# Entry to the convolution stage: a gate half scaled out of its bank into SBUF, two weight roundings moved behind a sigmoid, and the spread of the norm's factor two k steps earlier

## The chip, the cores and the metric

One core of one Trainium2 chip runs the whole program once. The metric is the device time in microseconds, the median of the runs shown. TensorE does matmuls, VectorE (DVE), ScalarE (ACT) and GpSimd (POOL) do elementwise work, and SyncE (SP) only issues the DMAs that bring weights.

## The reference

Two transformer-like blocks on 512 tokens of width 1024, in float32. The change touches the entry of each phase that begins with a root-mean-square norm, and above all the start of the conformer convolution:

```python
def conformer_conv(h, w_pw1, b_pw1, w_dw, b_dw, ln_g, ln_b, w_pw2, b_pw2):
    u = h @ w_pw1 + b_pw1                # 1024 -> 2048
    a, g = jnp.split(u, 2, axis=-1)
    u = a * jax.nn.sigmoid(g)
    u = depthwise_conv(u, w_dw) + b_dw   # 31 taps along the tokens
    u = jax.nn.silu(layer_norm(u, ln_g, ln_b))
    return u @ w_pw2 + b_pw2

# in the layer: h = rms_norm(x, gain); x = x + rms_norm(conformer_conv(h, ...), gain)
```

## The kernel before

Activations lie transposed, 128 channels by 512 tokens to a tile, eight tiles to a tensor. Every float32 product is made of three matmuls with rounded parts: the high part of the weight with the high and with the low part of the activation, and the low part of the weight with the high part (L1646, L1647, L1648). A k step of a tile is one such triple, and a tile of TensorE is eight k steps, 24 matmuls.

Weights come in blocks of 128x1024. For block n, SP loads `raw` once `w_lo` says that the block four back is done on GpSimd; ScalarE rounds it to the high part `wh` (`hi`, L631), once TensorE has finished the block four back (`blocks_done`); GpSimd subtracts and gets the low part `wl` (`lo`, here L528); then TensorE may use the block (`open_block` waits for `w_lo`). All rings have four places. Results go round PSUM banks 0 to 3: tile T waits until tile T-4 has been released by VectorE (`open_tile`, `bank_free`).

A phase with a norm begins with `enter` on TensorE: its first three tiles run interleaved over k, as the operand's pieces arrive, and the fourth follows as a whole. The norm is not applied to the operand but to the results. During the fourth tile, hooks put in the sum of squares (`stat`, ahead of k step 1) and, ahead of k step 5, `spread`, which spreads the factor (`rcol`, from VectorE's reciprocal, L1081) over all partitions in PSUM. ScalarE copies it to `r2` (`keep_r2`, L663), and VectorE multiplies results by `r2`. The kernel has five entries with hooks: the first MLP tiles of both layers, the convolution stage `pw1`, and two in the second block.

`pw1` works in the order of the list `PW1`: a0, g0, a1, g1, then for each j from 2 to 7: a_j, c_(j-2), g_j, and at the end c6, c7. a_j and g_j are the two halves of the projection for 128 channels, c_j is eight of the 31 taps as matmuls with diagonal weights. n0 is the first block of the stage, T0 its first tile, one block to each entry of the list. Each engine has its own program, in an order written out by hand:

- VectorE, for each j: `gate(j)` scales a_j (in place, in its bank) and g_j (into `tmp[:, 1]`, which signals `gate_z`) by `r2`, combines c_(j-2), and with the sigmoid makes U(j) (L1409). Then `taps(j)`: 18 taps (L1422 to L1434, by helpers at L1056 and L1060). The first of them releases the banks of both halves (2 for j<2, 3 after that, with c_(j-2)).
- ScalarE: for each g in the list the sigmoid (L879), the high part UH(j) (L883), then roundings of blocks up to four or five places ahead (L884, L885), and then five products for GpSimd's taps (L898). Before the list, `enter` (L689) rounds blocks n0+4 to n0+7.
- GpSimd: after `lo_to(n0 + 7)` (L569), for each j: the low part UL(j) (L556), blocks, tap additions (L539), blocks, tap additions, a running sum (L546), vector-tap additions (L567), blocks.
- TensorE: tile c0 is preceded by ten filler matmuls (L1656) and waits for UH(0) and UL(0).

Of the kernel before, what the change touches and what calls it, by code (L numbers as in the profile page):

```python
# [27 lines left out]
ALU = mybir.AluOpType  # L28
# [85 lines left out]
PW1_BLOCK, PW1_TILE = {}, {}  # L114
# [16 lines left out]
def build(nc, x_t, meta_t, positions, vectors, weights, out_t):  # L131
    ctx = ExitStack()
    with ctx:
        def sb(name, shape, dt=F32):
            return ctx.enter_context(nc.sbuf_tensor(name, shape, dt))

        def sem(name):
            return ctx.enter_context(nc.semaphore(name))
# [11 lines left out]
        tmp = sb("tmp", [P, 2, S])  # L150
# [3 lines left out]
        r2 = sb("r2", [P, S])  # L154
# [88 lines left out]
        PS = ctx.enter_context(nc.psum_tensor("PS", [P, 8, S], F32))  # L243
# [17 lines left out]
        def col(name, i=0):  # L261
            return vec[:, COL[name] + i:COL[name] + i + 1]
# [18 lines left out]
        blocks_done = sem("blocks_done")  # L281
        bank_free = sem("bank_free")
# [333 lines left out]
        def _(sc):  # L616
# [7 lines left out]
            def hi(n):  # L624
                if n >= NBLK:
                    return
                j = n % RING
                sc.wait_ge(raw_in[j], 16 * (n // RING + 1))
                if n >= RING:
                    sc.wait_ge(blocks_done, n - RING + 1)  # L630
                sc.activation(wh[:, j], raw[:, j], ACT.Copy).then_inc(w_hi, 1)  # L631
# [57 lines left out]
            def enter(phase, entry):  # L689
                n0 = BLOCK0[phase]  # L690
                hi(n0 + 4)
                root(entry)
                hi(n0 + 5)
                keep_r2(entry)
                hi(n0 + 6)
                hi(n0 + 7)
# [174 lines left out]

            boundary("x2")
            n0 = BLOCK0["pw1"]
            enter("pw1", "x2")
            done = n0 + 8
            for i, (kind, j) in enumerate(PW1):
                if kind == "g":
                    sc.wait_ge(gate_z, j + 1)
# [7 lines left out]
                done = max(done, upto)  # L886
# [30 lines left out]
            n0 = BLOCK0["w_in_2"]  # L917
# [91 lines left out]
            n0 = BLOCK0["ffn_up"]  # L1009
# [27 lines left out]
        def _(v):  # L1037
            chain = [0]

            def step(ins):  # L1040

                chain[0] += 1
                ins.then_inc(dve, 1)
                v.wait_ge(dve, chain[0])
# [6 lines left out]
            def tt(out, a, b, op):  # L1051
                return v.tensor_tensor(out, a, b, op)  # L1052

            def ts(out, a, s1, op0, s2=None, op1=None):
                if op1 is None:
                    return v.tensor_scalar(out, a, s1, None, op0)  # L1056
                return v.tensor_scalar(out, a, s1, s2, op0, op1)
# [93 lines left out]
            T0, n0 = TILE0["w_in"], BLOCK0["w_in"]  # L1151
# [215 lines left out]
            T0, n0 = TILE0["pw1"], BLOCK0["pw1"]  # L1367
# [26 lines left out]
            def gate(j):  # L1394

                b = j % 2
                Ta, Tg = T0 + PW1_TILE[("a", j)], T0 + PW1_TILE[("g", j)]
                a = PS[:, Ta % 4]
                v.wait_ge(blocks_done, n0 + PW1_BLOCK[("a", j)] + 1)
                step(tt(a, a, r2[:], ALU.mult))  # L1400
                v.wait_ge(blocks_done, n0 + PW1_BLOCK[("g", j)] + 1)
                tt(tmp[:, 1], PS[:, Tg % 4], r2[:], ALU.mult).then_inc(gate_z, 1)
                if j >= 2:
                    conv_out(j - 2)
                v.wait_ge(gate_s, j + 1)
                if j >= 2:
                    v.wait_ge(uh_done, j - 1)
                    v.wait_ge(ul_done, j - 1)
                sig(stt(U[:, b, PAD:PAD + S], a, col("b_pw1", j), sqb[:, 0], ALU.add, ALU.mult), u_done, j + 1)  # L1409

            def taps(j):

                b, first, end = j % 2, PE_TAPS, TAPS - POOL_TAPS
                Tg = T0 + PW1_TILE[("g", j)]
                base = chain[0]
                if j:
                    v.wait_ge(dve_taps, 2 * j)
                for t in range(first, end):
                    a = PS[:, (RB, HB)[t % 2]]
                    w, src = col("w_dw", j * TAPS + t), U[:, b, t:t + S]  # L1420
                    if t == first:
                        ts(a, src, w, ALU.mult).then_inc(bank_free, 2 if j < 2 else 3)  # L1422
                        continue
                    if t == first + 1:
                        ts(a, src, w, ALU.mult).then_inc(dve, 1)
                        continue
                    if t == first + 2:
                        v.wait_ge(bank_free, Tg + 1)
                    else:
                        v.wait_ge(dve, base + t - 2 - first)  # L1430
                    if t < end - 2:
                        stt(a, src, w, a, ALU.mult, ALU.add).then_inc(dve, 1)
                    else:
                        stt(taps_sum[:, b, t % 2], src, w, a, ALU.mult, ALU.add).then_inc(dve_taps, 1)  # L1434
                chain[0] += end - 3 - first
# [27 lines left out]
            T0, n0 = TILE0["w_in_2"], BLOCK0["w_in_2"]  # L1463
# [153 lines left out]
            T0, n0 = TILE0["ffn_up"], BLOCK0["ffn_up"]  # L1617
# [19 lines left out]
            T0, n0 = TILE0["ffn_down"], BLOCK0["ffn_down"]  # L1637
# [5 lines left out]
        def _(pe):  # L1643
# [22 lines left out]
            def stat(job):  # L1666

                n = JOB[job]
                pe.wait_ge(ssq_adds, SSQ_ADDS[n])
                if n:  # L1670
                    pe.wait_ge(sd_done, n)
                if job == "meta":
                    pe.matmul(PS[0:META, STAT, 0:1], ssq[:, 0:META], ones[:, 0:1], start=True, stop=True).then_inc(stat_done, 1)
                    return
                for j in range(4):
                    ins = pe.matmul(PS[:, STAT, j:j + 1], ssq[:, j * P:(j + 1) * P], ones[:, 0:1], start=True, stop=True)  # L1676
                ins.then_inc(stat_done, 1)

            def spread(job):

                n = JOB[job]
                pe.wait_ge(rcol_done, n + 1)
                if job == "meta":
                    pe.matmul(PS[:, RB, 0:META], rcol[0:META, n, 0:1].broadcast_to((META, P)), ident[0:META, 0:META],
                              start=True, stop=True).then_inc(rb_done, 1)
                    return
                for j in range(4):
                    ins = pe.matmul(PS[:, RB, j * P:(j + 1) * P], rcol[:, n, j:j + 1].broadcast_to((P, P)), ident[:],  # L1688
                                    start=True, stop=True)
                ins.then_inc(rb_done, 1)  # L1690
# [17 lines left out]
            def enter(phase, operand, hook_job=None):  # L1708

                n0, T0, x0 = BLOCK0[phase], TILE0[phase], KT * OPN[operand]  # L1710
                for k, t in [(k, t) for k in range(KT) for t in range(3)]:
                    if k == 0:
                        open_block(n0 + t)
                        open_tile(T0 + t)
                    if t == 0:
                        pe.wait_ge(xh, x0 + k + 1)
                        pe.wait_ge(xl, x0 + k + 1)
                    ins = products(PS[:, (T0 + t) % 4], *weight(n0 + t, k), XH[:, k], XL[:, k], k == 0, k == KT - 1)
                    if k == KT - 1:
                        ins.then_inc(blocks_done, 1)  # L1720
                hooks = {1: lambda: stat(hook_job), 5: lambda: spread(hook_job)} if hook_job else {}
                tile(n0 + 3, T0 + 3, hooks)

            def norm_out(job, next_phase, before=W_STAT, after=W_UPDATE):
# [57 lines left out]
            def spread_meta():  # L1782
# [3 lines left out]
            hooks = {4: {4: lambda: spread("x0"), 7: lambda: stat("q_lat")}, 5: {5: lambda: spread("q_lat")},  # L1786
                     6: {3: lambda: stat("kv_lat")}, 7: {2: lambda: spread_kv()},
                     9: {2: lambda: stat("meta")}, 12: {2: lambda: spread_meta()}}
# [11 lines left out]
            n0, T0 = BLOCK0["up_q"], TILE0["up_q"]  # L1800
# [4 lines left out]
            n0, T0 = BLOCK0["up_kn"], TILE0["up_kn"]  # L1805
# [4 lines left out]
            n0, T0 = BLOCK0["up_v"], TILE0["up_v"]  # L1810
            open_block(n0)
            for t in range(4):
                open_tile(T0 + t)
                q = slice(t * P, (t + 1) * P)
                for k in range(2):
                    w = [x[:, n0 % RING, 4 * k:4 * k + 4].rearrange("p s m -> p (s m)") for x in (wh, wl)]
# [84 lines left out]
            n0, T0 = BLOCK0["w_out"], TILE0["w_out"]  # L1901
# [38 lines left out]
            n0, T0 = BLOCK0["pw1"], TILE0["pw1"]  # L1940
# [49 lines left out]
            n0, T0 = BLOCK0["w_in_2"], TILE0["w_in_2"]  # L1990
# [46 lines left out]
            n0, T0 = BLOCK0["w_in_2b"], TILE0["w_in_2b"]  # L2037
# [3 lines left out]
            for i in range(4):  # L2041
# [4 lines left out]
                for kk in range(2):  # L2046
                    k = 2 * i + kk
                    w = [x[:, n % RING, 4 * kk:4 * kk + 4].rearrange("p s m -> p (s m)") for x in (wh, wl)]
# [15 lines left out]
            n0, T0 = BLOCK0["w_out_2"], TILE0["w_out_2"]  # L2064
# [5 lines left out]
            n0, T0 = BLOCK0["ffn_up"], TILE0["ffn_up"]  # L2070
# [8 lines left out]
            n0, T0 = BLOCK0["ffn_down"], TILE0["ffn_down"]  # L2079
# [163 lines left out]
```

## Time and profile before

| | us |
|---|---|
| median of 3 runs (1879.87 to 1881.52) | 1880.98 |
| the profiled execution | 1879.82 |
| its span in the profile | 1878.0 |
| TensorE busy | 1820.3 |
| GpSimd busy | 900.8 |
| VectorE busy | 809.6 |
| ScalarE busy | 636.8 |

The span runs from the first to the last instruction; the execution's own time has 1.8 us around it. Busy times are sums over the span of one execution. TensorE's granted clock is 0.985 of full speed over the span. A stretch of the stage in question is 665 to 800 us. Rows of a timeline give start and length in microseconds, engine, line, operation and tiles, and in brackets how long the engine was idle before it and what released it; short idle times have no bracket.

### The profile page before, as it was taken

To read this page: it belongs to the slowest core of one execution; us is meant where nothing else is said; L and a number is where in the kernel's file an instruction comes from. 1 tells how busy PE (TensorE), PEld (TensorE's weight loads), DVE (VectorE), ACT (ScalarE), POOL (GpSimd) and SP (SyncE) were. 2 spreads that over 40 slices of the span, in tenths; PEclk is the share of its full clock that TensorE was granted. 3 is DMA by queue.
4 is the path that set the end of the run, shared out by engine and by line. 5 is a ranking of instruction groups with operands and counts; after the bars stand their busy time and mean duration, and the time that the engine had idled before them with its cause. 6 is when DMAs were issued, how large, how long until landed. Compare 5 with 4: busy or idle time off the path is not lost.

```text
span 1878.0 us, 23679 instructions
## 1 busy us (share of the span) xinstructions
PE 1820.3 (97%) x8511; PEld 1506.6 (80%) x8511; DVE 809.6 (43%) x1238; ACT 636.8 (34%) x954; POOL 900.8 (48%) x478
## 2 busy tenths in 40 slices
PE   7999999999999989999999999998998999999999
PEld 5787887888888768787888888887878778888887
DVE  7447645301321478855520232256546154444200
ACT  5327525222321444444321222252245242222221
POOL 5346445444444479954444444453243354444443
PEclk9999999999999989999999999998999999999999
DMA  5332022233232213221322322310210223322332
GB/s 176 85 121 68 12 90 79 90 101 96 93 101 92 66 56 102 68 88 61 109 95 95 101 91 99 100 57 24 81 57 1 68 68 101 101 94 96 101 103 76
DMA packets 45925, 157.87 MB, mean 84 GB/s; under 512 B 5728, under 2 KB 5984, under 8 KB 45856
## 3 DMA queue, kind: packets, MB, share of 16 engines
q1 hardware_dynamic: 45856, 156.93, 26.4%
q8 instruction: 46, 0.75, 0.2%
q14 instruction: 23, 0.19, 0.0%
HBM read 152.58 MB, written 2.10 MB: 82 GB/s over the span
## 4 chain that ended last, share of the span: by engine, by line
PE 86%; POOL 5%; DVE 5%; issue 2%; ACT 2%; DMA 0%; SPq 0%; POOLq 0%; DVEq 0%; ACTq 0%
PE PS L1646 27%; PE PS L1647 26%; PE PS L1648 26%; POOL acc_p L539 2%; PE PS L1656 2%; POOL wl L528 2%; PE PS L1857 1%; PE PS L1688 1%; PE PS L1676 1%; DVE PS L1060 1%; POOL acc_p L567 1%; PE PS L2017 1%; POOL UL L556 0%; DVE tmp L1060 0%; DVE XL L1052 0%
## 5 line engine op out<-in xcount | busy, mean ns | idle before, releaser
L475 POOL TENSOR_TENSOR wl<-raw,wh 128x1024 fp32r<-128x1024 f32 x232 | 563.0, 2428 | 677.0 <-ACT wh L645 293.1
L1646 PE MATMUL PS<-XH,wh 128*128 128x512 f32 x1408 | 561.2, 399 | 14.8 <-DVE PS L1056 5.0
L1647 PE MATMUL PS<-XL,wh 128*128 128x512 f32 x1408 | 552.3, 392 | 0.0
L1648 PE MATMUL PS<-XH,wl 128*128 128x512 f32 x1408 | 551.9, 392 | 0.0
L1646 PEld LDWEIGHTS PS<-XH,wh 128*128 128x128 f32 x1408 | 267.0, 190 | 78.5 <-issue 12.4
L1648 PEld LDWEIGHTS PS<-XH,wl 128*128 128x128 f32 x1408 | 266.7, 189 | 56.9
L1647 PEld LDWEIGHTS PS<-XL,wh 128*128 128x128 f32 x1408 | 267.0, 190 | 52.6
L1646 PE MATMUL PS<-HH,wh 128*128 128x512 f32 x688 | 267.6, 389 | 0.0
L1647 PE MATMUL PS<-HL,wh 128*128 128x512 f32 x688 | 267.6, 389 | 0.0
L1648 PE MATMUL PS<-HH,wl 128*128 128x512 f32 x688 | 267.6, 389 | 0.0
L645 ACT ACTIVATE wh<-raw 128x1024 fp32r<-128x1024 f32 x96 | 101.6, 1061 | 405.0 <-PE PS L1648 405.0
L1052 DVE TENSOR_TENSOR tmp<-PS,r 128x512 f32<-128x512 f32 x116 | 79.9, 691 | 236.2 <-PE PS L1648 215.9
L631 ACT ACTIVATE wh<-raw 128x1024 fp32r<-128x1024 f32 x94 | 98.6, 1055 | 154.6 <-PE PS L1648 146.0
L1648 PEld LDWEIGHTS PS<-HH,wl 128*128 128x128 f32 x688 | 129.1, 188 | 26.8
L1646 PEld LDWEIGHTS PS<-HH,wh 128*128 128x128 f32 x688 | 129.1, 188 | 26.8
L1647 PEld LDWEIGHTS PS<-HL,wh 128*128 128x128 f32 x688 | 129.1, 188 | 26.8
L466 POOL TENSOR_TENSOR wl<-raw,wh 128x1024 fp32r<-128x1024 f32 x33 | 80.5, 2446 | 131.1 <-ACT wh L631 131.0
L864 ACT ACTIVATE wh<-raw 128x1024 fp32r<-128x1024 f32 x56 | 59.4, 1060 | 164.2 <-PE PS L1648 164.2
L1031 ACT ACTIVATE wh<-raw 128x1024 fp32r<-128x1024 f32 x40 | 42.5, 1062 | 159.0 <-PE PS L1648 159.0
L496 POOL TENSOR_TENSOR prob<-prob,cols 128x512 f32<-128x512 f32 (+2 forms) x64 | 57.5, 901 | 64.4 <-DVE cols L1266 64.1
L1356 DVE COPY M<-PS 128x512 f32 x16 | 11.1, 692 | 158.6 <-PE PS L1648 158.6
L1052 DVE TENSOR_TENSOR X<-X,PS 128x512 f32<-128x512 f32 x16 | 11.0, 687 | 148.5 <-PE PS L1648 148.5
(310 smaller groups left out, 2302.0 us busy)
## 6 DMA issues: line engine op xcount, KB each, us to landing
raw<-weights SPq DMA_DIRECT2D x286, 512.0 KB, 3.5
X<-x_t SPq DMA_DIRECT2D x8, 256.0 KB, 6.8
out_t<-X SPq DMA_DIRECT2D x8, 256.0 KB, 4.4
KH<-rope_h SPq DMA_DIRECT2D x4, 128.0 KB, 4.6
KL<-rope_l SPq DMA_DIRECT2D x4, 128.0 KB, 5.3
QH<-XH SPq DMA_DIRECT2D x16, 32.0 KB, 2.0
QL<-XL SPq DMA_DIRECT2D x16, 32.0 KB, 2.0
pos_i<-positions SPq DMA_DIRECT2D x1, 256.0 KB, 9.3
```

What stands on the lines that cost most here:

```text
L466: pool.tensor_tensor(wl[:, n % RING], raw[:, n % RING], wh[:, n % RING].bitcast(F32), ALU.subtract).then_inc(w_lo, 1)
L475: pool.tensor_tensor(wl[:, j], raw[:, j], wh[:, j].bitcast(F32), ALU.subtract).then_inc(w_lo, 1)
L496: pool.tensor_tensor(p, p, cols[:, u % 4, 2:3].broadcast_to(p.shape), ALU.mult).then_inc(p_done, 1)
L528: pool.tensor_tensor(wl[:, i % RING], raw[:, i % RING], wh[:, i % RING].bitcast(F32), ALU.subtract).then_inc(w_lo, 1)
L631: sc.activation(wh[:, j], raw[:, j], ACT.Copy).then_inc(w_hi, 1)
L645: sc.activation(wh[:, j], raw[:, j], ACT.Copy).then_inc(w_hi, 1)
L864: sc.activation(wh[:, slot], raw[:, slot], ACT.Copy).then_inc(w_hi, 1)
L1031: sc.activation(wh[:, slot], raw[:, slot], ACT.Copy).then_inc(w_hi, 1)
L1052: return v.tensor_tensor(out, a, b, op)
L1646: pe.matmul(out, wa, xa, start=start, stop=False)
L1647: pe.matmul(out, wa, xb, start=False, stop=False)
L1648: return pe.matmul(out, wb, xa, start=False, stop=stop)
```

## The change

There are four edits.

1. `gate(0)` on VectorE scales the first a-tile out of its bank into `tmp[:, 0]` by the helper `scaled` (L1115), which also releases the bank at once. U(0) is then made from `tmp[:, 0]`. For j of 1 and more all is as before.
2. The first tap of j=0 releases one bank instead of two.
3. ScalarE at the entry of `pw1`: the roundings of blocks n0+6 and n0+7 no longer stand in the entry; the loop over `PW1` issues them when its count reaches them.
4. In `enter` on TensorE the spread stands ahead of k step 3 instead of 5, for all five entries.

```diff
             boundary("x2")
             n0 = BLOCK0["pw1"]
-            enter("pw1", "x2")
-            done = n0 + 8
+            hi(n0 + 4)
+            root("x2")
+            hi(n0 + 5)
+            keep_r2("x2")
+            done = n0 + 6
             for i, (kind, j) in enumerate(PW1):
                 if kind == "g":
                     sc.wait_ge(gate_z, j + 1)
@@
                 b = j % 2
                 Ta, Tg = T0 + PW1_TILE[("a", j)], T0 + PW1_TILE[("g", j)]
-                a = PS[:, Ta % 4]
-                v.wait_ge(blocks_done, n0 + PW1_BLOCK[("a", j)] + 1)
-                step(tt(a, a, r2[:], ALU.mult))
+                a = PS[:, Ta % 4] if j else tmp[:, 0]
+                if j:
+                    v.wait_ge(blocks_done, n0 + PW1_BLOCK[("a", j)] + 1)
+                    step(tt(a, a, r2[:], ALU.mult))
+                else:
+                    scaled(a, Ta, n0 + PW1_BLOCK[("a", j)] + 1)
@@
                     if t == first:
-                        ts(a, src, w, ALU.mult).then_inc(bank_free, 2 if j < 2 else 3)
+                        ts(a, src, w, ALU.mult).then_inc(bank_free, (1, 2)[j] if j < 2 else 3)
                         continue
@@
-                hooks = {1: lambda: stat(hook_job), 5: lambda: spread(hook_job)} if hook_job else {}
+                hooks = {1: lambda: stat(hook_job), 3: lambda: spread(hook_job)} if hook_job else {}
                 tile(n0 + 3, T0 + 3, hooks)
```

## Rows read from the trace of the kernel before

**Rows 1.** The page, part 1: busy time, share of span, instructions of each engine.
```profile
PE 1820.3 (97%) x8511; PEld 1506.6 (80%) x8511; DVE 809.6 (43%) x1238; ACT 636.8 (34%) x954; POOL 900.8 (48%) x478
```

**Rows 2.** Waits of TensorE: engine, line, releaser: us in total, times, longest.
```profile
PE PS L1646 <- DVE PS L1056: 7.5, 2, 5.0
...
PE PS L1646 <- DVE PS L1060: 0.5, 2, 0.3
```

**Rows 3.** Timeline of TensorE, 660 to 690: spread, start of a2, fillers, c0.
```profile
662.38 1.05 PE L1688 MATMUL PS<-ident,rcol 128*128 128x128 f32 x8
...
670.49 0.76 PE L1646 MATMUL PS<-XH,wh 128*128 128x512 f32 x1 [4.98 <-DVE PS L1056]
...
678.79 2.43 PE L1656 MATMUL PS<-ident_r 128*128 128x512 f32 x10
681.06 0.39 PE L1646 MATMUL PS<-UH,wh 128*128 128x512 f32 x1
```

**Rows 4.** Timeline of TensorE, 727 to 787: first matmuls of g5, g6, g7.
```profile
740.50 0.40 PE L1646 MATMUL PS<-XH,wh 128*128 128x512 f32 x1
...
757.01 0.39 PE L1646 MATMUL PS<-XH,wh 128*128 128x512 f32 x1
...
773.82 0.51 PE L1646 MATMUL PS<-XH,wh 128*128 128x512 f32 x1
```

**Rows 5.** Windows: us, busy (x) of PE, PEld, DVE, ACT, POOL, PEclk, DMA share, GB/s.
```profile
663.27:701.05 37.78, 30.27 (x119) 24.07 (x118) 32.54 (x51) 16.13 (x23) 25.14 (x18) 0.90 0.18 57
...
735.85:753.60 17.75, 17.75 (x79) 14.54 (x78) 15.87 (x25) 8.53 (x13) 17.32 (x12) 1.00 0.29 90
```

**Rows 6.** Timeline of GpSimd, 645 to 830: lo(6), UL(0), lo(9), lo(21).
```profile
665.09 2.35 POOL L528 TENSOR_TENSOR wl<-raw,wh 128x1024 fp32r<-128x1024 f32 x1 [1.81 <-ACT wh L631]
670.25 1.35 POOL L556 TENSOR_TENSOR UL<-U,UH 128x542 fp32r<-128x542 f32 x1 [2.80 <-ACT UH L883]
...
701.05 2.39 POOL L528 TENSOR_TENSOR wl<-raw,wh 128x1024 fp32r<-128x1024 f32 x1 [1.58 <-ACT wh L631]
...
771.35 2.42 POOL L528 TENSOR_TENSOR wl<-raw,wh 128x1024 fp32r<-128x1024 f32 x1
```

**Rows 7.** Timeline of VectorE, 645 to 712: factor, scaling of g0, U(0).
```profile
659.89 0.18 DVE L1081 RECIPROCAL rcol<-sd 128x4 f32<-128x4 f32 x1 [4.84 <-ACT sd L657]
...
665.14 0.69 DVE L1052 TENSOR_TENSOR tmp<-PS,r 128x512 f32<-128x512 f32 x1
668.73 0.75 DVE L1060 SCALAR_TENSOR_TENSOR U<-PS,vec,sqb 128x512 f32<-128x512 f32 x1 [2.89 <-ACT sqb L879]
```

**Rows 8.** Instructions of L1060: duration ns min/median/max, first and last start, forms.
```profile
L1060 DVE SCALAR_TENSOR_TENSOR XL<-X,vec,XH x16: 739/1772/2875, 5.4 to 1520.8; 128x512 fp32r<-128x512 f32 x16
```

**Rows 9.** Timeline of all engines, 1535 to 1538.5, at the last entry.
```profile
1535.96 1.29 DVE L1052 TENSOR_TENSOR tmp<-PS,r 128x512 f32<-128x512 f32 x2 [4.21 <-ACT r L663]
1537.30 0.19 PEld L1646 LDWEIGHTS PS<-XH,wh 128*128 128x128 f32 x1 [0.54 <-DVE tmp L1052]
```

**Rows 10.** Timelines of ScalarE, 645 to 712, and of 1525 to 1532.
```profile
663.47 0.60 ACT L663 ACTIVATE r<-PS 128x512 f32<-128x512 f32 x1 [2.65 <-PE PS L1688]
...
666.68 1.28 ACT L879 ACT_TABLE_LOAD   x1
667.97 0.72 ACT L879 ACTIVATE sqb<-tmp,vec 128x512 f32<-128x512 f32 x1
...
684.42 0.66 ACT L883 ACTIVATE UH<-U 128x542 fp32r<-128x542 f32 x1 [0.82 <-DVE U L1060]
...
699.38 0.66 ACT L883 ACTIVATE UH<-U 128x542 fp32r<-128x542 f32 x1 [0.87 <-DVE U L1060]
699.94 1.99 ACT L631 ACTIVATE wh<-raw 128x1024 fp32r<-128x1024 f32 x2
...
1529.68 1.28 ACT L657 ACT_TABLE_LOAD   x1
1531.37 0.17 ACT L657 ACTIVATE sd<-PS 128x4 f32<-128x4 f32 x1 [0.40 <-PE PS L1676]
```

## The prediction

> **Names.** In the convolution stage `pw1` the weight blocks are numbered from n0. Blocks 0 to 3 are a0, g0, a1, g1, then 4 = a2, 5 = c0, 6 = g2, 7 = a3, 8 = c1, 9 = g3, and so on in threes to 21 = g7. hi(n) is ScalarE's rounding of block n (L631) and lo(n) GpSimd's remainder (L528). U(j), UH(j) and UL(j) are gated half j, its high part (ScalarE, L883) and its low part (GpSimd, L556).
>
> **What bounds the kernel now.** I read the page first, then TensorE's list of waits, then the timelines of the four engines over the place of the change. TensorE is busy 97% of the span [rows 1], so a change pays only through TensorE's waits, its clock, or whatever will feed it later. The list of waits has 7.5 us in two pieces for the first tap of VectorE (L1056), the longer 5.0, and 0.5 us in two pieces for a squared hidden tile [rows 2]. The 5.0 us is a2, which can't open its bank until the first tap of j=0 has released it: it starts at 670.49 after 4.98 us of idleness, so it was ready at 665.5. The tile then takes 8.3 us (670.49 to 678.79) [rows 3] where one at full speed takes 5.5 (three tiles in 740.50 to 757.01) [rows 4]: the clock was low after the pause, which cost 2.8 more.
>
> TensorE isn't alone, though. From 735.85 to 753.60 GpSimd is busy 17.32 of 17.75 us [rows 5], and it needs 17.75 us for what TensorE does in 16.5. At g7 TensorE has to wait: lo(21) runs 771.35 to 773.77 [rows 6] and the tile starts at 773.82 [rows 4]. So GpSimd begins this stage ahead, loses 1.25 us per channel tile, and its lead is gone by g7. From 701.05 on, **GpSimd's queue sets the end of the stage**, and any lateness there goes through to g7 in full.
>
> **Part 1, the bank released early.** The first a-tile is scaled out of its bank into tmp. It has the shapes of the scaling of g0 that follows it (0.69, from 665.14) [rows 7], only its output moves, so it costs nothing. The bank is free once it ends, before 665.14, and lo(4), lo(5) ended earlier than that (GpSimd is at lo(6) by 665.09 [rows 6]). a2 then starts at 665.5 at full clock: the 4.98 and the 2.8 disappear here, but whether they are gained depends on the next tile, c0.
>
> U(0) now reads both operands from SBUF. VectorE's nearest such rows (XL from X) take 0.739 at best, 2.875 at worst [rows 8]; the worst would add 2.1. GpSimd reads and writes SBUF too, and it will be idle at that moment (its next work hangs on hi(6), below), so I take 0.74 and no cost. The Trainium skill (SBUF — State Buffer, the section on engine-side ports) speaks against this edit: a VectorE instruction with two SBUF inputs and a GpSimd instruction share one pair of ports, and the later one waits for the whole of the other. By that rule the edit would pay up to a lo here, if one ran; none does.
>
> **Part 2, the spread two k steps earlier.** It starts at 662.38, after five k steps [rows 3]. Two k steps are six matmuls of 0.23 = 1.38, so it starts at 661.0; what it needs, rcol, ends at 660.07 [rows 7], so no new wait. The four other entries are built alike. Here both scalings on VectorE, the second at 665.14 [rows 7], and r2 (ScalarE, 663.47, below) go 1.38 earlier: the second scaling ends at 664.45. At the four other entries the same edit removes what TensorE waits after its fourth tile: 0.5 us for two of them together (the layers' first MLP tiles) [rows 2], and 0.3 at the last (the pair of scalings ends at 1537.25; the weight load of TensorE's next tile starts at 1537.30 after 0.54 of waiting [rows 9], and loads run ahead of matmuls by about a matmul, 0.23). At the fourth entry no wait follows, and I take nothing. Sum: **-0.8**, bounds -0.9 and 0.
>
> **Part 3, hi(6) and hi(7) moved behind a sigmoid.** Before, they run ahead of the first sigmoid, then comes the table load (666.68), then the sigmoid at 667.97 and U(0) at 668.73 [rows 7, 10]. With both gone from there, ScalarE goes from r2 (ends 662.7) straight to the table load. Elsewhere the load doesn't wait for its activation's data: at 1529.68 it runs although the root it serves starts at 1531.37 [rows 10]. So it is over at 664.0, and the sigmoid starts with its data at 664.49. U(0) follows 0.76 later as now, at 665.25: **3.48 earlier** than 668.73. Were the load to wait for the data, it would be 1.28 less. The Trainium skill (ScalarE: Activation LUTs, What ACT_TABLE_LOAD costs) adds a drain of about 1.38 us to each load; here the sigmoid starts 0.01 us after the load ends [rows 10], so the trace doesn't show it, and by it U(0) would come some 0.9 later.
>
> Now where they go. ScalarE's loop runs over a0, g0, a1, g1 and so on with index i, and at a g it issues the roundings below block i+5, at another entry those below i+4 (L884). At g0, i=1, that is below block 6, which `done = n0 + 6` already covers: **nothing is issued behind the first sigmoid**. At a1 the limit is 6 again. Only g1 (i=3) has 8, and at g1 ScalarE first waits for the second gate's data, its sigmoid and U(1). All of that is behind VectorE's 18 taps of j=0. So hi(6) comes right after UH(1), which is at 684.42 now and 3.48 earlier then, 680.94. A hi follows UH by 0.56, and the lo follows it by 1.11 (699.38, 699.94, 701.05) [rows 6, 10], so lo(6) starts at **682.6** instead of 665.09.
>
> GpSimd's queue puts lo(6) ahead of UL(0) (`lo_to(n0 + 7)`, then `low_u(0)`). Behind the new wait stand UL(0), for which c0 on TensorE waits, and then all the tap sums and lows of the stage. UL(0), 670.25 now [rows 6], starts at 682.6 + 2.37 = 685.0 and ends at 686.3. TensorE: a2 665.5 to 671.0, the ten filler matmuls 2.27 (678.79 to 681.06) [rows 3] to 673.3, then idle for **13.1 us** until 686.4. c0 follows at low clock, for which I take the 2.8 of the present restart; bounds 0 and 4.8 a tile (24 times 0.43 less 0.23, a tile wholly at low clock).
>
> GpSimd meanwhile: what it does from lo(6) to lo(9) is 3 lows, 2 UL, 8 tap additions and 4 vector-tap additions, 25.14 us of busy time between 663.27 and 701.05, where 12.6 us were waits [rows 5]. Run without pauses, at the ratio of 17.75 to 17.32, that is 25.8. And it runs so: VectorE's tap sums come 3.48 earlier than now; hi(8) follows the products of j=1 at about 693, well before lo(8); hi(9) follows UH(2), which follows g2 (ends 700.2, below), at about 703; and the load of block 10, which SP holds back until lo(6) is done at 685, has until then too. lo(9) starts at 682.6 + 25.8 = 708.4 against 701.05 [rows 6]: **+7.4**. From there its queue is the same and full, so lo(21) ends at 781.2, and g7 starts there instead of at 773.82 [rows 4].
>
> TensorE alone: c0 from 686.4 to 694.7 (5.5 and 2.8), g2 to 700.2, then from g2's start 16.5 per three tiles: g7 at 777.2. That is before 781.2, so GpSimd's queue decides, with 4.0 us over for a dearer restart. I expect waits at g4, g5, g6, g7 of at most 1.3 each.
>
> **Sum.** +7.4 at g7, carried to the end of the stage, and -0.8 at the other entries: **+6.6 us**. The profiled execution is 1879.82 (span 1878.0), 1.16 below the median 1880.98. It becomes 1886.4, and the median **1887.6**, +0.35%.
>
> **Rivals.**
> - *The lows follow the first sigmoid after all* (I misread the list; the change does what its name says). hi(6) would run at about 666.6, lo(6) at 667.7, UL(0) would end at 671.4, ahead of c0 at 673.3. TensorE would run through to c1, which waits for the first tap of j=2 as now [rows 2], 3.48 earlier; lo(9), behind UH(2), also. -3.5 - 0.8 = -4.3: **1876.7**, faster. It decides if hi(6) is issued before the second gate's wait. Only the name of the change speaks for it; the indices speak against. 0.04.
> - *GpSimd's delay is absorbed and TensorE sets the pace*: place, GpSimd's queue from lo(9) to lo(21); it decides if its period falls to 16.5 or less. Then g7 is at 777.2, +3.4, in all +2.6: **1883.6**, no measurable change. For it: TensorE waits for a lo only at g7 now. Against it: 17.32 busy of 17.75 [rows 5]. 0.05.
> - *The long pause costs more clock*: c0 and g2 wholly at low clock, 9.6 instead of 2.8, put TensorE's g7 at 784.0, behind GpSimd's. +10.2 - 0.8 = +9.4: **1890.4**. For it: the pause is 13.1 us, not 5.0. Against it: after 4.98 the clock was back within one tile. 0.06.
>
> **How the numbers follow.** The forecast has 0.85 and its own range is 1886.0 (GpSimd's 25.1 instead of 25.8, and 0.9 for the medians) to 1889.6 (the table load waits, +1.28, and 0.7 for the medians). The 8-in-10 range is 1885.2 to 1890.2: it adds the other entries' bound of 0 above, something for the sum of many small steps below, and nearly reaches the clock rival. A measurement of this kernel can tell about 0.2%, 3.8 us, from no change. Slower by more: forecast and clock rival, 0.90. Same: the absorbed delay, and a small share, 0.05. Faster: 0.05.
>
> **What would show it.** Right: a2 starts at about 665.5 with no wait; TensorE idles about 13 us before c0 and waits for UL(0); two L631 run just behind the second UH at about 681; GpSimd is idle from 663.3 to 682.6; lo(9) starts at about 708.4; g7 at about 781.2, after growing waits for L528. Wrong: an L631 between the first UH and the taps' products near 667, a GpSimd period under 17 us, or gates g4 to g7 that don't wait.

## The result and the profile after

The changed kernel takes 1886.51 us (median of 20 runs, 1884.53 to 1888.97) against 1881.09 (20 runs of the kernel before). The ratio is 1.0027 with an interval of 1.0019 to 1.0035: slower by 0.27%. The forecast was 1887.6, or +6.6; the interval of the ratio is +3.6 to +6.6. The ratio compares means and the differences in microseconds compare medians, and in the experiments below the two don't agree to the microsecond, because 18 of the 80 executions of the kernel before took 5 to 9 us more than its median at a lower granted clock (0.978 to 0.982), which none of the 105 executions of kernels with the early release of the bank shows.

The profiled execution of the changed kernel has a span of 1887.2 us, 9.2 more than before. Some of that is not the change's. These are TensorE's waits in the first 40 us, before any edited instruction, in the kernel before and then in the changed one (in total, times, longest):

```profile
PE PS L1656 <- ACT ident_r L700: 3.0, 1, 3.0
PE PS L1739 <- DVE XL L1060: 2.9, 2, 2.2
PE PS L1739 <- ACT wh L631: 0.2, 1, 0.2
```
```profile
PE PS L1662 <- ACT ident_r L700: 3.0, 1, 3.0
PE PS L1745 <- DVE XL L1063: 2.7, 2, 2.4
PE PS L1745 <- ACT XH L705: 1.6, 1, 1.6
PE PS L1745 <- ACT wh L631: 1.4, 1, 1.4
```

The first weight block landed later in this execution (its rounding starts at 7.10, not at 5.90), and the reciprocal of the entry (rcol, 659.89 before) is at 662.28. So I measure every trace from its own rcol. The chain that the prediction followed, after it:

VectorE (timeline of the changed kernel, as all fences until the experiments):
```profile
662.28 0.18 DVE L1084 RECIPROCAL rcol<-sd 128x4 f32<-128x4 f32 x1 [4.86 <-ACT sd L657]
665.15 0.24 DVE L1372 MEMSET U<- 128x30 f32 x2 [2.69 <-ACT r L663]
665.42 1.42 DVE L1055 TENSOR_TENSOR tmp<-PS,r 128x512 f32<-128x512 f32 x2
667.63 0.75 DVE L1063 SCALAR_TENSOR_TENSOR U<-tmp,vec,sqb 128x512 f32<-128x512 f32 x1 [0.79 <-ACT sqb L882]
```
ScalarE:
```profile
664.48 0.60 ACT L663 ACTIVATE r<-PS 128x512 f32<-128x512 f32 x1 [1.27 <-PE PS L1694]
665.09 1.28 ACT L882 ACT_TABLE_LOAD   x1
666.87 0.72 ACT L882 ACTIVATE sqb<-tmp,vec 128x512 f32<-128x512 f32 x1 [0.50 <-DVE tmp L1055]
...
683.26 0.66 ACT L886 ACTIVATE UH<-U 128x542 fp32r<-128x542 f32 x1 [0.82 <-DVE U L1063]
683.82 1.99 ACT L631 ACTIVATE wh<-raw 128x1024 fp32r<-128x1024 f32 x2
```
GpSimd:
```profile
663.28 2.38 POOL L528 TENSOR_TENSOR wl<-raw,wh 128x1024 fp32r<-128x1024 f32 x1 [0.46 <-ACT wh L631]
684.94 2.36 POOL L528 TENSOR_TENSOR wl<-raw,wh 128x1024 fp32r<-128x1024 f32 x1 [19.27 <-ACT wh L631]
687.25 1.33 POOL L556 TENSOR_TENSOR UL<-U,UH 128x542 fp32r<-128x542 f32 x1
...
711.25 2.39 POOL L528 TENSOR_TENSOR wl<-raw,wh 128x1024 fp32r<-128x1024 f32 x1
...
781.43 2.38 POOL L528 TENSOR_TENSOR wl<-raw,wh 128x1024 fp32r<-128x1024 f32 x1
```
TensorE, the fillers, c0, and the first matmuls of g3 to g7:
```profile
673.16 2.43 PE L1662 MATMUL PS<-ident_r 128*128 128x512 f32 x10
688.69 0.77 PE L1652 MATMUL PS<-UH,wh 128*128 128x512 f32 x1 [13.09 <-issue]
...
713.70 0.50 PE L1652 MATMUL PS<-XH,wh 128*128 128x512 f32 x1 [0.82 <-POOL wl L528]
...
730.73 0.50 PE L1652 MATMUL PS<-XH,wh 128*128 128x512 f32 x1 [0.29 <-POOL wl L528]
...
748.45 0.51 PE L1652 MATMUL PS<-XH,wh 128*128 128x512 f32 x1 [0.93 <-POOL wl L528]
...
766.16 0.50 PE L1652 MATMUL PS<-XH,wh 128*128 128x512 f32 x1 [0.94 <-POOL wl L528]
...
783.87 0.51 PE L1652 MATMUL PS<-XH,wh 128*128 128x512 f32 x1 [0.93 <-POOL wl L528]
```

To read it: both roundings (683.82) stand behind the second high part (683.26), not behind the first sigmoid (666.87). GpSimd waits 19.27 us for them, with UL(0) queued behind, and TensorE 13.09 us for UL(0); the view calls that releaser "issue", but c0 starts 0.1 us after UL(0) ends (688.58). The wait of 4.98 at a2 [rows 3] is gone. In its place stand 13.09 at c0, for UL(0), then 0.8 at g3 and 0.3 to 0.9 at each g after it, for a lo each time. From 748.45 to 783.87 the gates are 17.7 us apart, GpSimd's period [rows 5], not TensorE's 16.5 [rows 4].

Milestones from each trace's own rcol, in us, of all runs; g7 is the start of that tile on TensorE, "end" is the end of the span. The last column is the median against that of the kernel before in the same comparison (10 to 12 executions of each kernel, 7 of e10 and 6 of e9, against 12 to 35 of the kernel before). Below, two kernels of different comparisons are set against each other by this column.

| kernel | U(0) | lo(6) | lo(9) | lo(21) | g7 | end | median, difference |
|---|---|---|---|---|---|---|---|
| before | 8.84 | 5.20 | 41.16 | 111.46 | 113.93 | 1218.11 | |
| changed | 5.35 | 22.66 | 48.97 | 119.15 | 121.59 | 1224.92 | +5.4 |
| e1_parts_early | 5.35 | 7.82 | 37.61 | 107.91 | 110.38 | 1214.42 | -3.4 |
| e2_no_move | 8.83 | 3.82 | 41.10 | 111.40 | 113.83 | 1217.80 | -0.9 |
| e3_move_alone | 6.73 | 24.10 | 50.36 | 120.52 | 122.95 | 1228.30 | +7.9 |
| e4_ul_first | 5.35 | 22.66 | 47.56 | 117.70 | 120.14 | 1224.56 | +5.5 |
| e5_taps_first | 5.34 | 22.65 | 39.23 | 109.60 | 112.04 | 1215.30 | -3.0 |
| e6_filler | 5.35 | 22.66 | 49.03 | 119.18 | 121.61 | 1224.88 | +6.4 |
| e7_relieved_before | 8.83 | 5.19 | 41.17 | 108.21 | 113.64 | 1218.19 | +0.2 |
| e8_relieved_after | 5.35 | 22.66 | 48.96 | 115.98 | 118.43 | 1221.67 | +3.0 |
| e10_packed | 5.35 | 7.82 | 31.49 | 107.06 | 110.09 | 1214.85 | -3.7 |
| e9_packed_a2 | 5.35 | 7.82 | 31.53 | 105.86 | 108.29 | 1211.35 | -8.3 |

### The profile page after: what moved, and what is told of

It reads as the page before. It is cut to its first block, busy times and chain, and to the rows that moved or that the text cites. A ratio compares the mean times of both kernels' runs of the same rounds, so it can differ in the third digit from the quotient of the medians.

```text
span 1887.2 us, 23678 instructions
## 1 busy us (share of the span) xinstructions
PE 1818.1 (96%) x8511; PEld 1504.9 (80%) x8511; DVE 810.2 (43%) x1238; ACT 637.1 (34%) x954; POOL 901.2 (48%) x478
## 4 chain that ended last, share of the span: by engine, by line
PE 85%; POOL 5%; DVE 5%; issue 2%; ACT 2%; DMA 0%; SPq 0%; POOLq 0%; ACTq 0%; DVEq 0%
PE PS L1652 27%; PE PS L1653 26%; PE PS L1654 26%; POOL acc_p L539 2%; PE PS L1662 2%; POOL wl L528 2%; PE PS L1863 1%; POOL acc_p L567 1%; PE PS L1682 1%; PE PS L1694 1%; POOL UL L556 1%; DVE XL L1063 1%; DVE PS L1063 1%; PE PS L2023 1%; DVE tmp L1063 0%
```

## The experiments

**Is it the place of the two roundings?** The first run puts them where the name of the change has them, behind the first high part, with all else as changed (UH(0) starts 0.8 us after the first sigmoid has ended).

```diff
-                upto = n0 + i + (5 if kind == "g" else 4)
+                upto = n0 + i + ((7 if j == 0 else 5) if kind == "g" else 4)
```

> The changed kernel, but blocks n0+6 and n0+7 are rounded right behind the first high part UH(0), ahead of the tap products, so nothing waits for the second gate. Theory (GpSimd's queue, late by 7.5 us at lo(9), sets the end of the stage): that lateness is gone, lo(9) starts 3.5 us earlier than in the kernel before, and the time is about 4.3 us under the kernel before, 10 to 11 under the changed one. Rival (the loss comes from the other edits: U(0) reading two SBUF tiles, or the early spread): it stays 5 to 7 us above the kernel before.

1877.03 us, -3.4, ratio to before 0.9975 (0.9964 to 0.9986). That is 8.8 us under the changed kernel in the medians and 10.5 in the traces' ends. lo(9) is 3.55 earlier than before, the end 3.7. The place of the two roundings is what turns a gain of some 0.2% into a loss. TensorE's new waits, at g2 and at c1, are for banks:

```profile
682.72 0.47 PE L1652 MATMUL PS<-XH,wh 128*128 128x512 f32 x1 [3.03 <-DVE PS L1059]
...
697.58 0.57 PE L1652 MATMUL PS<-UH,wh 128*128 128x512 f32 x1 [2.09 <-DVE PS L1059]
```

**What are the other edits worth without the move?** Edit 3 undone (the entry calls `enter("pw1", "x2")` and `done = n0 + 8` again).

> The changed kernel with edit 3 undone: the roundings of n0+6 and n0+7 stand in the entry again; the early release of the bank and the early spread stay. Theory: a2 starts without its 5 us wait, but the first sigmoid still stands behind the rounding of n0+7, which waits for g1, so U(0) comes when it did and the first tap of j=2 and lo(9) too: TensorE's wait moves from a2 to c1 (some 10 us there instead of 2.5), and only 0.7 us are gained, from the other entries. Rival (TensorE's stall at a2 is what costs): 5 to 8 us are gained.

1879.60, -0.9, ratio 0.9989 (0.9976 to 1.0001), not told from no change. a2 no longer waits, and the wait is back further on (its timeline of TensorE, g2 and c1):

```profile
684.72 0.76 PE L1649 MATMUL PS<-XH,wh 128*128 128x512 f32 x1 [6.52 <-DVE PS L1056]
...
699.59 0.50 PE L1649 MATMUL PS<-UH,wh 128*128 128x512 f32 x1 [1.46 <-DVE PS L1056]
```

6.52 and 1.46 make 8.0, against 7.5 in two waits before [rows 2]. I expected some 10, all of it at c1. The place was wrong: g2 needs a1's bank, which the first tap of j=1 releases, so most of it stops there and not at c1. U(0) and lo(9) are where they were, and so is the time. The 5 us wait at a2 was slack of TensorE against VectorE's and GpSimd's lists.

The mirror image is edit 3 alone, on the kernel before.

> The kernel before with edit 3 alone: the roundings of n0+6 and n0+7 move into the loop; the bank of a0 is released by the first tap as before and the spread stays where it was. Theory: U(0) comes 2.1 us earlier than before, so the second gate and lo(6) come 1.4 us later than in the changed kernel; about 8.8 us above the kernel before, 2.2 above the changed one. Rival (the first edits add to the loss): 5 us or less above the kernel before.

1888.17, ratio 1.0035 (1.0022 to 1.0048), +7.9; in the trace lo(21) is 9.1 later and the end 10.2. The expected 8.8 lies between the 7.9 of the medians and the 10.2 of the trace, and the loss is larger than with all four edits, as expected: the early spread gives U(0) 1.4 back.

**TensorE's stall or GpSimd's queue?** The trace of the changed kernel has a wait of 13 us on the busiest engine, and this is where a reader would look. Three runs take away the stall, its low clock, or the queue behind it. First only UL(0) goes ahead of lo(6):

```diff
-            lo_to(n0 + 7)
+            lo_to(n0 + 6)
+            low_u(0)
+            lo_to(n0 + 7)
             for j in range(KT - 1):
                 n = n0 + PW1_BLOCK[("g", j)]
-                low_u(j)
+                if j:
+                    low_u(j)
```

> The changed kernel, but GpSimd makes UL(0) before lo(6) instead of after it, so that c0 needn't wait for the second gate. Theory: c0 starts at once after the fillers, g2 waits for lo(6) in its place, and lo(9) comes only the 1.3 us of UL(0) earlier: about 5.3 us above the kernel before, 1.3 under the changed one, although TensorE's stall is only half as long. Rival (TensorE's 13 us stall sets the loss): about 7 us under the changed kernel.

1885.95, +5.5, ratio 1.0022 (1.0013 to 1.0032). c0 doesn't wait at all; g2 waits 6.16 us for lo(6), half the stall, and lo(9) is 1.41 earlier than in the changed kernel. TensorE isn't done with waiting, though: a3 waits for lo(7), which still stands behind the additions of j=0:

```profile
699.90 0.79 PE L1655 MATMUL PS<-XH,wh 128*128 128x512 f32 x1 [3.83 <-POOL wl L528]
```

g7 is 1.45 earlier, as lo(9) is; the end in the trace only 0.4. The medians can't tell e4 from the changed kernel; what they exclude is the rival's 7 us.

Then the stall is filled, so that the clock stays up:

```diff
-                keep_busy(W_GATE if j == 0 else 0, PS[:, T % 4])
+                keep_busy(W_GATE + 57 if j == 0 else 0, PS[:, T % 4])
```

> The changed kernel with 57 more filler matmuls ahead of c0 (67 instead of 10), which last about as long as TensorE's stall there and hold its clock up. Theory (GpSimd's queue decides, TensorE has 4 us to spare): the low clock after the stall costs nothing in the end, and the time is that of the changed kernel within 0.5 us. Rival (the clock after the stall is part of the loss): 2.8 us less than the changed kernel.

1886.64, +6.4, ratio 1.0023 (1.0010 to 1.0036): as slow as the changed kernel (+5.4), and not 2.8 under it. The ends of the two traces agree to 0.04 us. The clock did stay up. This is the stretch behind the stall, first in the changed kernel, then here (busy times by engine, the third from the end is the granted clock, 0.50 being 1.2 GHz):

```profile
688.60:692.70 4.10, 4.01 (x10) 3.17 (x11) 4.10 (x8) 1.45 (x2) 3.78 (x3) 0.50 0.34 123
```
```profile
686.70:691.00 4.30, 4.29 (x19) 3.51 (x20) 4.30 (x7) 1.69 (x3) 3.87 (x4) 1.00 0.29 113
```

What the clock gave back, TensorE waited away: its waits for lows (L528) rose from 3.9 to 5.4 us, and g3 starts at 51.45 from rcol against 51.42. The low clock cost nothing here, as the tiles from g3 on wait for a lo in either case.

Third, the roundings stay late, the stall stays half (6.17 us at g2), but GpSimd does UL(0) and all additions of j=0 in the time in which it waits:

```diff
-            lo_to(n0 + 7)
-            for j in range(KT - 1):
+            lo_to(n0 + 6)
+            low_u(0)
+            add_taps(0, 1, POOL_TAPS)
+            add_vector_taps(0)
+            lo_to(n0 + 7)
+            for j in range(1, KT - 1):
```

> The changed kernel, but GpSimd does UL(0), the four tap additions and the two vector-tap additions of j=0 before lo(6), in time in which it only waited. Its queue from lo(6) to lo(9) is then 16.4 us long instead of 25.8. Theory: lo(9) starts 2 us earlier than in the kernel before, and the time is about 2.8 us under the kernel before, although lo(6) is as late as in the changed kernel (17 us after its old place) and g2 waits about 6 us for it. Rival (the late roundings themselves cost, through TensorE): 3 us or more above the kernel before.

1877.50, -3.0, ratio 0.9979 (0.9968 to 0.9989). lo(6) is at 22.65, as late as in the changed kernel, and lo(9) at 39.23, 1.9 before its old time. Its GpSimd timeline:

```profile
667.36 1.36 POOL L556 TENSOR_TENSOR UL<-U,UH 128x542 fp32r<-128x542 f32 x1 [3.48 <-ACT UH L890]
668.68 5.61 POOL L539 TENSOR_TENSOR acc_p<-acc_p,tapped 128x512 f32<-128x512 f32 x4
677.98 2.71 POOL L567 TENSOR_TENSOR acc_p<-acc_p,taps_sum 128x512 f32<-128x512 f32 x2 [3.69 <-DVE taps_sum L1067]
683.15 2.36 POOL L528 TENSOR_TENSOR wl<-raw,wh 128x1024 fp32r<-128x1024 f32 x1 [2.46 <-ACT wh L635]
...
699.73 2.43 POOL L528 TENSOR_TENSOR wl<-raw,wh 128x1024 fp32r<-128x1024 f32 x1
```

e4 and e5 have the same first stall on TensorE, 6.16 and 6.17 us at g2, and differ by 8.5 us in their medians. Their programs differ only in the order of GpSimd's list: in e4 lo(7) and lo(9) come late as well (hence its 3.83 at a3), in e5 they don't.

**Does the full queue carry the lateness to the end?** The same part of the running sum, 1.1 us for each channel tile, is left out of both kernels. Both lack most of the sum behind the layer norm's mean.

```diff
-                    pool.tensor_tensor(sum1[:], sum1[:], conv[:, j], ALU.add).then_inc(sum1_done, 1)
+                    pool.tensor_tensor(sum1[:, 0:8], sum1[:, 0:8], conv[:, j, 0:8], ALU.add).then_inc(sum1_done, 1)
```

> The kernel before, with GpSimd's running sum of the convolution's tiles (the part of the layer norm's mean) done on 8 of 512 columns from the second tile on, which leaves most of that sum out: 1.2 us less on GpSimd for each channel tile. Theory: TensorE's wait at g7 (0.3) and at the last sum (0.6) go: about 1 us under the kernel before.

> The changed kernel with the same part of the running sum left out. GpSimd's period falls from 17.75 to about 16.5 us, TensorE's own pace. Theory (lateness at lo(9) costs in full only because the queue is full from there to g7): the lateness doesn't grow after g3, g7 comes 3.8 us later than with the relieved kernel before, and the two relieved kernels are 3.0 us apart instead of 6.6. Rival (the stall alone costs, whatever the queue): still 5 us or more apart.

1880.47 and 1883.25, ratios to before 1.0003 (0.9990 to 1.0016) and 1.0006 (0.9995 to 1.0017): 2.8 apart in the medians (3.5 in the traces' ends), against 5.4 (6.8) with the full sum. The two ratios can't tell the relieved kernels apart, so the split below rests on the traces. GpSimd's period in the second is nearly TensorE's own, 16.69 us against 16.5 (window from lo(15) to lo(18)):

```profile
742.44:759.13 16.69, 16.69 (x74) 13.55 (x73) 14.71 (x24) 7.36 (x11) 16.26 (x13) 1.00 0.30 95
```

The starts of g5, g6 and g7 follow it:

```profile
744.92 0.50 PE L1652 MATMUL PS<-XH,wh 128*128 128x512 f32 x1
...
761.59 0.51 PE L1652 MATMUL PS<-XH,wh 128*128 128x512 f32 x1
...
778.26 0.50 PE L1652 MATMUL PS<-XH,wh 128*128 128x512 f32 x1
```

Against its own kernel before, g3 is 3.8 us late with the full sum and without it (51.42 and 51.40 against 47.60 and 47.61 from rcol). By g7 this has grown to 7.7 with the full sum and only to 4.8 without. I had 3.8 at g7: GpSimd is still a little slower than TensorE (16.67 us between those starts, 16.51 in e7), and each of them comes right after a lo. So half of the loss is the stall that TensorE can't make up, and most of the other half is made by a queue slower than TensorE. On the kernel before, the relief was worth nothing (+0.2, where I expected -1): lo(21) comes 3.3 earlier, but TensorE gains only its 0.3 at g7, and at the end of the stage it waits for the last convolution tile of VectorE in place of the sum.

**A version that beats both.** First the queue alone: on e1, lo(7), lo(8), lo(9) are moved ahead into waits of GpSimd.

```diff
-                upto = n0 + i + ((7 if j == 0 else 5) if kind == "g" else 4)
+                upto = n0 + i + ((7 if j == 0 else 6 if j == 1 else 5) if kind == "g" else 4)
+                if i == 5:
+                    upto = n0 + 10
...
-                lo_to(n + 5)
+                lo_to((n0 + 8, n0 + 9)[j] if j < 2 else n + 5)
...
+                if j == 1:
+                    lo_to(n0 + 10)
                 add_vector_taps(j)
```

> The kernel with the two roundings right behind the first sigmoid, and GpSimd's early waits filled besides: lo(7) stands before the tap additions of j=0, lo(8) before those of j=1, lo(9) before the vector-tap additions of j=1, and ScalarE rounds n0+8 and n0+9 as early as their places are free. GpSimd is then 3.5 us further ahead after lo(9). Theory: in that kernel TensorE's own waits for banks at g2 (3.0) and c1 (2.1) bound it as closely as GpSimd's queue does, so the lead is worth little: 0 to 0.5 us beyond it, 4.5 us under the kernel before. Rival (GpSimd's queue alone decides): 3.5 us beyond it, 7 us under the kernel before.

1876.40, ratio 0.9965 (0.9950 to 0.9980): -3.7, which is 0.3 us beyond e1, where the rival wanted 3.5; g7 is 0.3 earlier than in e1, too. lo(10) is 3.3 earlier than in e1 and lo(12) only 0.8: the queue waits again (2.45 us before lo(12)), now for ScalarE's rounding, which stands behind the high part of the gate and so behind TensorE and VectorE. Then the bank as well:

```diff
-                a = PS[:, Ta % 4] if j else tmp[:, 0]
-                if j:
+                a = tmp[:, 0] if j == 0 else sqb[:, 1] if j == 2 else PS[:, Ta % 4]
+                if j == 2:
+                    pass
+                elif j:
...
-                        ts(a, src, w, ALU.mult).then_inc(bank_free, (1, 2)[j] if j < 2 else 3)
+                        ts(a, src, w, ALU.mult).then_inc(bank_free, (1, 2, 2)[j] if j < 3 else 3)
+                        if j == 1:
+                            scaled(sqb[:, 1], T0 + 4, n0 + 5)
```

> The same packed queue, and VectorE scales a2 out of its bank into sqb behind the first tap of j=1, so that c1 needn't wait for the first tap of j=2. Theory: with both limits moved, c1 starts about 4.7 us earlier than it would and lo(9) isn't late for g3; 3.5 us beyond the kernel with the roundings behind the first sigmoid, about 7.5 us under the kernel before. Rival (U(2), which now reads two SBUF tiles while GpSimd works, waits for it and takes up to 2.4 us longer, or the scaling in the midst of the taps delays the second gate): 5 us or less under the kernel before.

1871.84 (6 executions), ratio 0.9950 (0.9936 to 0.9964): 8.3 us under the kernel before and 13.7 under the changed one; its interval ends where that of e1 begins (0.9964). In the traces the gain on the kernel before is smaller, 5.6 at g7 and 6.8 at the end, and g7 is 2.1 earlier than in e1 and 1.8 earlier than in e10. Two of the seven executions of e10 (1871.28 and 1871.92) are as fast as e9's, so how much the bank itself gives is known only roughly. Behind the wait at c1 the granted clock of e10's trace is 0.50 for about 3.4 us, while e9's is 1.00 over the same tiles, so part of the gain may be clock. c1 no longer waits. g2 still waits 3.04 us for a bank, c2 now waits for one, and g7 again for a lo:

```profile
709.51 0.50 PE L1660 MATMUL PS<-UH,wh 128*128 128x512 f32 x1 [2.14 <-DVE PS L1063]
...
766.04 0.50 PE L1660 MATMUL PS<-XH,wh 128*128 128x512 f32 x1 [0.93 <-POOL wl L528]
```

## Why the prediction was right

The steps of the prediction happened in their order: nothing is issued behind the first sigmoid, so lo(6) waits for the second gate, and GpSimd's full queue carries its lateness to g7. The experiments e1, e4, e5, e6 and e8 each bear on one of these steps. The steps came within 0.5 us, but for the extra time of c0 (0.7 off), which decides nothing, and a wait at g3 that wasn't foreseen.

Point by point, in us from rcol, predicted and measured in the changed kernel:

- U(0): 5.36, and 5.35. The table load runs ahead of its data (665.09, behind it ScalarE waits 0.50 for tmp), and no drain is seen after it: from the end of r2 (665.08) to the start of the sigmoid (666.87) are 1.79 us for load, drain and wait together. So the row decided rightly against the 1.38 that the Trainium skill gives for the drain (ScalarE: Activation LUTs, What ACT_TABLE_LOAD costs).
- The edited U(0), with two SBUF operands, takes 0.75; GpSimd waits at that time (665.66 to 684.94).
- lo(6): 22.7, and 22.66. That is the reading of the loop's indices, and the step with most weight: e1, which issues them one gate sooner, takes 8.8 us less.
- TensorE's stall at c0: 13.1, and 13.09. The low clock behind it cost 2.1 us (c0 takes 7.5, from 688.69 to 696.21, for its 5.5), less than the 2.8 that I took from the present restart; e6 shows that it decides nothing.
- lo(9): +7.4, and +7.8. I had 25.8 us of queue, it was 26.3 (22.66 to 48.97). The vector-tap additions start 0.15 us behind the additions before them, not at once.
- g7: +7.4, and +7.7 (121.59 against 113.93). The waits at g4 to g7 were 0.3, 0.9, 0.9, 0.9. There is one at g3 that I didn't have, 0.8, since the queue came a little later and c0 a little sooner than reckoned.
- The other entries: -0.8. The two waits behind the first MLP tiles (0.5) [rows 2] are gone from the changed kernel's list, and from lo(21) to the end of the span the trace is 0.9 shorter. The medians can't tell so little, and in e1 the same stretch is only 0.1 shorter. All traces together bear it out: from g7 to the end the nine kernels with the early spread take 1103.1 to 1104.8 us (mean 1103.7), the three without it 1104.2 to 1105.4 (mean 1104.7).
- The sum: +6.6 predicted, +6.8 in the traces from rcol on, +5.4 between medians, with 3.6 to 6.6 as the interval. The 1.4 us between trace and medians I can't place; it is within what single executions differ by.

The rivals: that the roundings follow the first sigmoid was excluded by the trace, and e1 gave its time (-3.4 for -4.3). That the lateness is absorbed is what e8 shows in large part once the queue is shortened (2.8 above e7 for +2.6; at g7, 4.8 for 3.4), so the mechanism was priced about rightly and is not there in the full kernel. The clock is excluded by e6.

## What to carry to other kernels

A step moved "behind" an operation in one engine's list has also moved behind every wait that stands between; count the list's indices for the first items, where a rule such as "up to i+5" can be satisfied already and issue nothing. Then look whose queue the moved step feeds: the long wait on the busiest engine was in plain sight here, but filling it, or moving half of it to later tiles, changed nothing that the medians can tell, while reordering an engine that is 48% busy over the span, and full in this stage, was worth 8.5 us. An engine whose period in a stage is longer than that of the engine it feeds has a lead that it spends; here 7.8 us taken from that lead came back as 7.7 at the last consumer. Lead added beyond what other limits allow is lost again (3.3 us at lo(10) were 0.8 at lo(12) in e10).

## What the runs showed of the hardware

VectorE's gate with two SBUF inputs and an instruction of GpSimd did meet in e9_packed_a2, where U(2) reads two SBUF tiles while GpSimd adds (timelines of GpSimd and VectorE):

```profile
691.64 3.16 POOL L567 TENSOR_TENSOR acc_p<-acc_p,taps_sum 128x512 f32<-128x512 f32 x2
```
```profile
692.89 0.75 DVE L1067 SCALAR_TENSOR_TENSOR U<-sqb,vec 128x512 f32<-128x512 f32 x1 [0.19 <-DVE conv L1067]
```

U(2) took its usual 0.75; the pair of additions took 3.16 us where such pairs take 2.69 to 2.77 elsewhere, so 0.4 was paid by GpSimd. Taken singly, the first addition ends at 692.94, 0.05 after U(2) has started; the second starts at 693.09, while U(2) runs until 693.64, and takes 1.71 us instead of 1.30. The Trainium skill (SBUF — State Buffer, the section on SBUF's two sides) has whichever starts first hold the shared ports for its whole instruction. The meeting agrees in who pays; the second addition paid 0.41 of the 0.55 us of U(2) that were left.

The kernel before has larger meetings, in the rows behind the prediction's 0.739 to 2.875 [rows 8]. XL from X at 9.87 runs with no instruction of GpSimd beside it and takes 0.74. Those at 7.60, 11.35, 13.64 and 16.42 start while GpSimd makes a low, take 2.35, 2.37, 2.86 and 2.88, and each ends 0.55 us after the low that was running (9.40, 13.17, 15.95 and 18.76). So here the later one does wait for the other's end. U(0) met nothing of GpSimd's, and U(2) met an addition that was almost over.

Of the clock: the granted clock fell to 0.50 (1.2 GHz) within the pause of 4.98 us in the kernel before, and the first 5.9 us of a2 ran at it. In the changed kernel it fell within the pause of 13.09, and the first 4.1 us of c0 ran at it. The extra time was 2.8 us for a2 and 2.1 for c0, so the long pause cost no more than the short one.
